# Where the split weights and the summed tokens of a seven-product matmul group start in SBUF, modulo 128 bytes

## Time and profile before

| what | us |
|---|---|
| median of 3 runs | 1020.42 |
| lowest and highest run | 1019.67, 1022.19 |
| span of the profiled execution, first to last instruction | 1018.0 |
| two stretches of seven-product groups | 76.1 to 253.4, 706.3 to 883.7 |

### The profile page before, as it was taken

One profiled execution on the slowest core, in us unless ns is written; L12 is line 12 of the kernel. 1 busy time (PEld: TensorE's weight loads), 2 busy tenths in 40 slices (PEclk: granted clock), 3 DMA queues, 4 the chain that ended last, 5 costly groups with the idle time before them and its releaser, 6 DMA issues.

```text
span 1018.0 us, 18544 instructions
## 1 busy us (share of the span) xinstructions
PE 996.2 (98%) x6942; PEld 867.3 (85%) x6942; DVE 747.5 (73%) x1039; ACT 506.2 (50%) x690; POOL 227.3 (22%) x191
## 2 busy tenths in 40 slices
PE   8999999999999999999999989999999999999997
PEld 6779999999888888786677767878999999988887
DVE  6778778777787868779899995566778777683334
ACT  5545444455332134578977973465444444433221
POOL 0024453543112301100100000202444544200100
PEclk9999999999999999999999999999999999999999
DMA  9557667674788836421121202235676676552322
GB/s 353 211 171 205 167 201 182 180 211 149 254 284 288 309 103 234 154 83 62 63 84 43 83 23 81 86 119 142 167 214 185 177 213 166 186 180 89 104 83 84
DMA packets 63190, 162.21 MB, mean 159 GB/s; under 512 B 5440, under 2 KB 7760, under 8 KB 63008
## 3 DMA queue, kind: packets, MB, share of 16 engines
q1 hardware_dynamic: 44720, 110.79, 30.4%
q0 software_dynamic: 18416, 50.68, 20.3%
HBM read 159.36 MB, written 2.10 MB: 159 GB/s over the span
## 4 chain that ended last, share of the span: by engine, by line
PE 90%; DVE 4%; ACT 3%; issue 2%; DMA 1%; SPq 0%; DVEq 0%; ACTq 0%
PE psum L1889 15%; PE psum L1891 15%; PE psum L1890 15%; PE psum L1961 12%; PE psum L1963 12%; PE psum L1962 12%; PE psum L2219 1%; PE psum L2256 1%; PE psum L2262 1%; PE psum L2190 1%; PE psum L2107 1%; PE psum L2192 1%; PE psum L2191 1%; PE psum L2276 1%; DVE wlo L1107 1%
## 5 line engine op out<-in xcount | busy, mean ns | idle before, releaser
L586 ACT ACTIVATE whi<-raw 128x1024 fp32r<-128x1024 f32 x92 | 97.2, 1057 | 227.7 <-PE psum L1891 211.0
L1107 DVE TENSOR_TENSOR wlo<-raw,whi 128x1024 fp32r<-128x1024 f32 x94 | 117.7, 1253 | 120.9 <-ACT whi L586 120.6
L1891 PE MATMUL psum<-ghi,wlo 128*128 128x512 f32 (+2 forms) x384 | 143.7, 374 | 0.0
L1890 PE MATMUL psum<-glo,whi 128*128 128x512 f32 (+2 forms) x384 | 143.4, 373 | 0.0
L1889 PE MATMUL psum<-ghi,whi 128*128 128x512 f32 (+2 forms) x384 | 143.0, 373 | 0.0
L1889 PE MATMUL psum<-hhi,whi 128*128 128x512 f32 x320 | 130.8, 409 | 2.0 <-DVE wlo L1107 1.3
L1891 PE MATMUL psum<-hhi,wlo 128*128 128x512 f32 x320 | 125.0, 391 | 0.0
L1890 PE MATMUL psum<-hlo,whi 128*128 128x512 f32 x320 | 124.9, 390 | 0.0
L1961 PE MATMUL psum<-forms,whi 128*128 128x256 f32 x432 | 121.1, 280 | 0.0
L1962 PE MATMUL psum<-forms,whi 128*128 128x256 f32 x432 | 120.5, 279 | 0.0
L1963 PE MATMUL psum<-forms,wlo 128*128 128x256 f32 x432 | 120.5, 279 | 0.0
(11 more groups left out here) (270 smaller groups left out, 2349.4 us busy)
## 6 DMA issues: line engine op xcount, KB each, us to landing
raw<-wu SPq DMA_DIRECT2D x96, 512.0 KB, 3.4
ada<-wada POOLq DMA_DIRECT2D x56, 512.0 KB, 5.1
sraw_a<-ws SPq DMA_DIRECT2D x36, 512.0 KB, 6.1
raw<-ws SPq DMA_DIRECT2D x36, 512.0 KB, 6.1
sraw_b<-ws SPq DMA_DIRECT2D x36, 256.0 KB, 3.9
sraw_a<-ws POOLq DMA_DIRECT2D x18, 512.0 KB, 6.0
raw<-ws POOLq DMA_DIRECT2D x18, 512.0 KB, 5.9
early<-wada SPq DMA_DIRECT2D x16, 512.0 KB, 15.3
```

The source lines that it names most:

```text
L586: nc.scalar.activation(whi[:, slot, :], raw[:, slot, :], ACT.Copy).then_inc(hi_done, 1)
L1107: nc.vector.tensor_tensor(wlo[:, slot, :], raw[:, slot, :], whi[:, slot, :], ALU.subtract).then_inc(lo_done, 1)
L1890: nc.tensor.matmul(dst, a, rlo, start=False, stop=False)
L1891: return nc.tensor.matmul(dst, b, rhi, start=False, stop=stop)
```

## The change

`hi4` and `lo4` become tiles of their own that overlap `whi` and `wlo`, 64 bytes further on; the two slots of each now lie 4,224 bytes apart. `whi` and `wlo` stay on multiples of 128 for `three`. `forms` starts 64 bytes later. The third row of `hix` and `lox` becomes a tile of its own, `hiy` and `loy`, and each of the four tiles is put 64 bytes further than the chain would. `g2` starts 64 bytes later as well. From the code, the new start bytes are: hi4 73,920 and 78,144 (slots), lo4 82,496 and 86,720, whi 73,856 and 78,080, wlo 82,432 and 86,656, ghi2 99,264, forms 107,520, hix 156,736, hiy 160,896, lox 163,008, loy 167,168, g2 169,280. The accesses of `group_upper`, `group_lower` and `product` follow; no instruction, wait or DMA is added or taken away.

```diff
--- before.py
+++ after.py
@@ -38,6 +38,8 @@
 N_MOD = 9
 EPS = 1e-6
 UNIT = KD * P
+HALF_LINE = 64
+GAP = HALF_LINE // 2
 HALF_UNITS = KF // 2
 PAIR_UNITS = HALF_UNITS - 4
 LEVELS = (64, 32, 16, 8, 4, 2, 1)
@@ -116,8 +118,14 @@
         hhi = sb("hhi", [P, KD, T], F32R)
         hlo = sb("hlo", [P, KD, T], F32R)
         raw = sb("raw", [P, 2, UNIT])
-        whi = sb("whi", [P, 2, UNIT], F32R)
-        wlo = sb("wlo", [P, 2, UNIT], F32R)
+        hi4w, _ = at("hi4", [P, 2, UNIT + GAP], F32R, place[0] + HALF_LINE)
+        whiw = sb("whi", [P, 2, UNIT + GAP], F32R)
+        place[0] += 2 * HALF_LINE
+        lo4w, _ = at("lo4", [P, 2, UNIT + GAP], F32R, place[0] + HALF_LINE)
+        wlow = sb("wlo", [P, 2, UNIT + GAP], F32R)
+        place[0] += 2 * HALF_LINE
+        whi, wlo = whiw[:, :, 0:UNIT], wlow[:, :, 0:UNIT]
+        hi4, lo4 = (w[:, :, 0:UNIT].rearrange("p u (q n) -> p u q n", q=2) for w in (hi4w, lo4w))
         vecs = sb("vecs", [P, N_VEC])
         ident = sb("ident", [P, P])
         ones = sb("ones", [P, P])
@@ -147,7 +155,7 @@
 
         off = arena
         ghi2, _ = at("ghi2", [P, KF, T], F32R, off)
-        forms, off = at("forms", [P, 4, 2, KD // 2 * HT], F32R, off + PLAIN * T * 4)
+        forms, off = at("forms", [P, 4, 2, KD // 2 * HT], F32R, off + PLAIN * T * 4 + HALF_LINE)
         xs, off = at("xs", [P, 2, T], F32, off)
         sraw_a0, off = at("sraw_a0", [P, 4, T], F32, off)
         sraw_b0, off = at("sraw_b0", [P, T], F32, off)
@@ -155,11 +163,13 @@
         csr, _ = at("csr", [P, D], F32, off - 4 * D)
         ada = tuple(at(f"ada{i}", [P, D], F32, a)[0] for i, a in
                     enumerate((off - 12 * D, off - 8 * D, off, off + 4 * D)))
-        hix, off = at("hix", [P, 3, T], F32R, off)
-        lox, off = at("lox", [P, 3, T], F32R, off)
+        hix, off = at("hix", [P, 2, T], F32R, off + HALF_LINE)
+        hiy, off = at("hiy", [P, T], F32R, off + HALF_LINE)
+        lox, off = at("lox", [P, 2, T], F32R, off + HALF_LINE)
+        loy, off = at("loy", [P, T], F32R, off + HALF_LINE)
         sraw_a = (sraw_a0, raw[:].rearrange("p u (q n) -> p (u q) n", q=2))
         sraw_b = (sraw_b0, sraw_b1)
-        g2_at = off
+        g2_at = off + HALF_LINE
         g2, off = at("g2", [P, KF, T], F32, g2_at)
         glo2, _ = at("glo2", [P, KF, T], F32R, g2_at)
         h32, t_at = at("h32", [P, KD, T], F32, g2_at + PLAIN * T * 4)
@@ -384,8 +394,6 @@
 
             return psum[:, 5 - 4 * s:7 - 4 * s, :].rearrange("p b (h t) -> p (b h) t", h=2)
 
-        hi4 = whi[:].rearrange("p u (q n) -> p (u q) n", q=2)
-        lo4 = wlo[:].rearrange("p u (q n) -> p (u q) n", q=2)
         h_left, h_right = h32[:, :, 0:HT], h32[:, :, HT:T]
 
         def tokens(i, k):
@@ -708,12 +716,12 @@
                     act.wait_ge(third_loaded[s], 16 * j + 16)
                 if part < 2:
                     act.wait_ge(sum_loaded[s], 16 * j + 16)
-                    src, dst = sraw_a[s][:, 2 * part:2 * part + 2, :], hi4[:, 2 * part:2 * part + 2, :]
+                    src, dst = sraw_a[s][:, 2 * part:2 * part + 2, :], hi4[:, part]
                 elif part == 2:
                     act.wait_ge(xs_done, 4 * j + (2 * s + 2))
-                    src, dst = xs[:], hix[:, 0:2, :]
+                    src, dst = xs[:], hix[:]
                 else:
-                    src, dst = sraw_b[s][:], hix[:, 2, :]
+                    src, dst = sraw_b[s][:], hiy[:]
                 nc.scalar.activation(dst, src, ACT.Copy).then_inc(shi_done, 1)
 
             def first_copy(j, s):
@@ -1351,11 +1359,11 @@
                 if part == 1:
                     dve.wait_ge(xs_done, 4 * j + (2 * s + 1))
                 if part < 2:
-                    src, up, dst = (t[:, 2 * part:2 * part + 2, :] for t in (sraw_a[s], hi4, lo4))
+                    src, up, dst = sraw_a[s][:, 2 * part:2 * part + 2, :], hi4[:, part], lo4[:, part]
                 elif part == 2:
-                    src, up, dst = xs[:], hix[:, 0:2, :], lox[:, 0:2, :]
+                    src, up, dst = xs[:], hix[:], lox[:]
                 else:
-                    src, up, dst = sraw_b[s][:], hix[:, 2, :], lox[:, 2, :]
+                    src, up, dst = sraw_b[s][:], hiy[:], loy[:]
                 nc.vector.tensor_tensor(dst, src, up, ALU.subtract).then_inc(slo_done, 1)
 
             def middle_sums(j, s):
@@ -1954,7 +1962,10 @@
                 if i == 6:
                     pe.wait_ge(p1_copied, 2 * j + (s + 1))
                 dst = sum_bank(i, s)
-                up, low = (hi4[:, i, :], lo4[:, i, :]) if i < 4 else (hix[:, i - 4, :], lox[:, i - 4, :])
+                if i < 4:
+                    up, low = hi4[:, i // 2, i % 2], lo4[:, i // 2, i % 2]
+                else:
+                    up, low = (hix[:, i - 4, :], lox[:, i - 4, :]) if i < 6 else (hiy[:], loy[:])
                 for k in range(KD // 2):
                     a, b = up[:, k * P:(k + 1) * P], low[:, k * P:(k + 1) * P]
                     rhi, rlo = tokens(i, k)
```

## The result

The change made the kernel slower: 1025.15 us, median of 11 runs (1023.07 to 1028.73), against 1020.83 for the kernel before in the same rounds (11 runs, 1019.67 to 1027.09). The ratio is 1.0046, with a 95% interval of 1.0032 to 1.006. The prediction said 1012.0 us with a range of 1009.5 to 1020.6: wrong in sign, and outside its range.

What follows compares the result with a forecast made beforehand. TensorE's matmul spacing, set by operand start addresses, was taken as the bound. Product terms summed to 0.23 us gained a group, 8.4 us in 36, taking the span from 1018.0 to 1009.6; time 1012.0 us, range 1009.5 to 1020.6.

Steps and rivals of the forecast that it cites:

- number 4 of its list: wlo, slot 1 and tiles behind move by multiples of 128; 512-column matmuls keep their remainders, so their starts stay unchanged.
- The terms of B21, NT3 and B12: In each seven-product group: B21 gains 0.06 us, NT3 together with T1 and NT4 0.16, B12 0.02.
- (64,0): Start remainders modulo 128 of weights and tokens; the cheapest pair at 256 columns, 113.3 ns a matmul, 1.36 us a product.
- T1, NT4 and T2: Products of each group, forecast at 1.36 us each; T1 and NT4 gain 0.16 us together with NT3, T2 0.07.
- I price it at nothing, with up to 1 us of one-off waits: Supply of weights to the groups: expected to keep up with 9.62 us a group, at no cost beyond that bound.
- rival D: Supply binds the groups at about 9.75 us each: gain 3.6 us, 1016.8 us; chance 0.08.
- The ring's slack: GpSimd's loop of sum, sum, accumulating DMA, landing: 9.59 us a group, just under the forecast 9.62.
- Rival A: Distance weights minus tokens counts modulo more than 128; groups gain 4.0 us, total 1018.2 to 1022.4 us; chance 0.14.
- Rival B: Slower end of Rival A's mechanism: 512-column matmuls held at the dearest 233.5 ns, 1028.5 us; chance 0.12.
- B's point of decision: Rival B decides once the 2,016 long matmuls lose over 2.0 ns each on average.
- Rival C: Addresses do not part the products; position or PSUM bank does: 1020.4 us; chance 0.06.
- the 24 us: Most the change could give, with groups at 9.17 us by the skill page's formula, 109.2 ns at 256 columns.

Runs made afterwards that it cites:

- e1_plain: Against the changed kernel, the seven-product groups' distances put back as before, only the plain matmul tiles left changed; 1027.68 us, ratio 1.0067.
- e3_256: Against e2_seven, both halves of six products at +64 modulo 256, B11 at 0, down projection still at -64; 1028.4 us, ratio 1.007.
- e4_third: Against e3_256, B11 at +64 too, so all seven products; same program as e4_again; 1026.12 us in its one run.
- e6_alt: Against e2_seven, all seven products with upper weights at +64 and lower at -64, down projection at distance 0; 1009.43 us, ratio 0.9905.
- e4_again: Against e3_256, B11 at +64 too, so all seven products; a repeat of an earlier kernel; 1025.69 us, ratio 1.0043.
- e8_best: The program of e6_alt run again, no edit; 1012.28 us, median of 6, ratio 0.9894.
- e2_seven: Against the changed kernel, the plain matmul tiles' distances put back as before, the seven-product groups left changed; 1022.21 us, ratio 1.0011.
- e7_zero_t2: Distances of e3_256, but the one product at 0 is T2 and not B11; 1010.84 us, ratio 0.9917.
- run 427: Not a label of a run: a verb and a time, the first output-projection matmuls starting 427 ns apart at a granted clock of 0.50.

## Why the prediction was wrong, by its own steps

- **The failed step is number 4 of its list**: wlo, slot 1 and everything behind move by "all multiples of 128. The 512-column matmuls keep their remainders", so their time was put at no change. It took the remainder modulo 128 for the whole of the matter. Slot 0 of wlo (384 bytes), slot 1 of whi (128) and glo2 (1,152) moved by odd multiples of 128, their partners by even ones or not at all, and e1_plain, which has that alone, shows the loss: 226.7 to 232.6 ns on hhi, 228.8 to 232.7 on ghi2. In after it costs 1.8 us in each down projection, 1.7 in the second up projection and some 2.6 in mixing.
- **The terms of B21, NT3 and B12 failed for the same reason.** Upper and lower halves now stand an odd multiple of 128 bytes apart, so "(64,0)" was two things. And no fixed price a pair would have done: the +64 that had given 113.3 ns in before gave 117.8 in e3_256, because the pace also goes by what ran before. B21 gained 0.04 us and not 0.06, NT3 nothing, B12 lost 0.05 where 0.02 of gain stood. T1, NT4 and T2 came to 1.36 as forecast, B11 to 1.43 for 1.44. A group gained 0.10 us for 0.23.
- **"I price it at nothing, with up to 1 us of one-off waits"** was too little for the profiled run, where the first stage lost 3.6 us; rival D in part. The ring's slack was worked out from one quiet stretch of the second stage, while its first ring steps depend on when an accumulating DMA lands. e4_third and e6_alt have no wait in the same stretch, e4_again and e8_best, the same programs, have one, so it is part of the spread of the runs; whether it is in the median run of after is not known.
- **Rival A had the right doubt**: that the rows could not settle whether more than 128 counts, as every start was at 128 or 192 modulo 256. Its 4.0 us for the groups stand against 3.6, in part by luck: T1, NT4 and T2 came out faster than it had them (113.3 ns for 114.8), B21, NT3 and B12 slower. NT3 and B12 were slower than T1, as it said. It sized the long matmuls at 1.8 to 6.0 us of loss; stretch by stretch it was about 8. Its own rule fell with e3_256. Rival B gave 8.5 us to the 1,248 on hhi and yhi and 3.6 to the 768 of the down projections. The count of 768 is 192 short: a group of rows with no width beside it (x64 on each of the three lines) has 512 columns too, so there are 960, and 2,208 long matmuls in all. 5.9 and 3.9 ns give 7.4 and 3.7 us; the stretches lost less because some of the long matmuls in the first up projection and in mixing ran above 226.7 ns in before already. B's point of decision, 2.0 ns a matmul, was passed.
- **Rival C falls**: addresses alone moved e1_plain by 0.67% and e6_alt by -0.95%. The Trainium skill, "SBUF — State Buffer", section "Who interferes with whom", has TensorE's two reads independent; these runs speak against it by up to 6.7 ns a matmul.
- The chances gave 0.12 to slower. A step that rests on "these keep their remainders" carried all the long matmuls, 2,016 by its count, against 3,024 shorter ones that were to gain; what the rows could not tell (modulo 128 or more) weighed on the larger part of the time and was given 0.26.

What stays open: what in the chip makes an order of loads and matmuls keep itself up, and which entry leads to which; whether a change of the granted clock shifts the order by itself; whether address bits above the lowest eight matter; and why an accumulating DMA lands 2 us late in the first stage of some executions (after, e2_seven, e8_best, e4_again) and not of others. "Order" is a name for what the starts show, a pace that holds; its cause was not seen. In e7_zero_t2 each load starts 2 to 4 ns behind a matmul at either pace (722.7 to 723.9 and 732.5 to 733.7); at the slower one a part of the loads takes 192 ns instead of 188.

## What to carry to other kernels

When a change of layout is said to leave an operand "at the same remainder", ask modulo what, and list the start of every operand of every matmul with the distance between its two parts; a region behind an inserted gap is part of the change. Before believing a price per address pair, look whether the same pair has the same price in another stage, or behind a wait: here it did not, and one profiled run can show either. The layout to take from this is e6_alt's: upper halves 64 bytes ahead of the tokens and lower halves 64 behind (modulo 256) for the 256-column matmuls, distance 0 for the 512-column ones; it beat both kernels in two sets of runs (ratios 0.9905 and 0.9894; e7_zero_t2, at 0.9917, is not told apart from it), and what its slowest profiled run lost was lost to the supply of the first stage and the low clock behind it.

## What the runs showed of the hardware

- The pace of float32r matmuls with a load each depends on where both operands start: 113.3 to 120 ns at 256 columns, 226.7 to about 234 at 512, at a granted clock of 1.00 in those stretches.
- At a distance of 64 bytes it also depends on history: 117.8 or 113.3 ns at 256 columns (e4_again, 9.89 and 9.52 us a group), 233.3 or 228.8 at 512 (e2_seven, e4_again), through a whole stage or up to a break. At 512 columns the pace went by that of the groups just ahead (e4_again: 229 ns behind 9.52, 233.3 behind 9.89).
- With +64 for the upper and -64 for the lower halves, the groups of e6_alt, and those of e8_best clear of a wait, took 9.52 us, 113.3 ns a matmul (9.54 for the first of a stage). The Trainium skill, "TensorE: Matmul & The Clock Gate", section "Back-to-back issue gap", gives N / 2.4 + 2.5 ns for the isolated gap of a single matmul, 109.2 at 256 columns and 215.8 at 512, and says that in a stream of loads and matmuls both set the spacing. The best rows here, of such a stream, stay 4 and 11 ns above the formula; the 24 us that the prediction took from it as the most there is to gain were thus no bound of the page's for this stream.
- Behind TensorE's gaps among the products of the scans the first output-projection matmuls sometimes run 427 ns apart, at the lower clock, granted 0.50 (after, e1_plain, e3_256, e8_best), and sometimes at some 231 from the second step on, at 1.00 (before, e6_alt): some 1.2 us.
- In the first stage of groups the granted clock fell to 0.50 for 3.4 us at the end of waits of 2.1 to 3.5 us or within 0.9 us behind them (e4_again, e2_seven, e8_best); in after, with waits of 1.4 and 1.7 us, it stayed at 1.00.
- In the first stage of groups the accumulating DMAs into sraw_a landed after 5.9 to 6.3 us in one execution of a program (e6_alt) and after 7.7 to 8.8 in another (e8_best).
